# Four reorderings inside in-order engine queues of a two-block transformer kernel

## The reference

```python
h = rmsnorm(x, ffn_pre_norm[l])
u = causal_depthwise_conv(h @ w_up[l], conv_w[l], conv_b[l])
gate, up = jnp.split(u, 2, axis=-1)
y = (jax.nn.gelu(gate, approximate=True) * up) @ w_down[l]
x = x + rmsnorm(y, ffn_post_norm[l])
```

```python
shift_m, scale_m, gate_m, shift_f, scale_f, gate_f = ada_mod(c, ada_w[layer], ada_b[layer])
h = modulate(rms_norm(x, norm_gains[layer, 0]), shift_m, scale_m)
x = x + gate_m * mixer(h)
h = modulate(rms_norm(x, norm_gains[layer, 1]), shift_f, scale_f)
x = x + gate_f * swiglu(h, ffn_w_gate_up[layer], ffn_w_down[layer])
```

## Time and profile before

| | |
|---|---|
| median of 3 runs | 1071.52 us |
| time of the profiled execution | 1071.52 us |
| its span, first to last instruction | 1069.7 us |
| PE busy | 1038.4 us, 97% |
| ACT busy | 589.0 us, 55% |
| POOL busy | 153.1 us, 14% |
| granted TensorE clock, mean | 0.993 |

### The profile page before, as it was taken

How to read it: one execution, slowest core, us unless ns; L and a number is a source line. 1 busy time by engine, 2 the same in 40 slices (tenths; PEclk the granted TensorE clock), 3 DMA queues, 4 the chain that set the end, 5 groups by cost and what they waited for, 6 DMA issues and landing times.

```text
span 1069.7 us, 20330 instructions
## 1 busy us (share of the span) xinstructions
PE 1038.4 (97%) x7901; PEld 986.4 (92%) x7901; DVE 809.5 (76%) x1392; ACT 589.0 (55%) x1015; POOL 153.1 (14%) x162
## 2 busy tenths in 40 slices
PE   7999999999999999999999999999999999999997
PEld 6987798999888997899999999988899999999997
DVE  5867689999997987588999788885558567675453
ACT  6686467666536675675444445533466456544442
POOL 0000033333201200023111011200000113111010
PEclk8999999999999999999999999999999999999999
DMA  9642245777695443257998788454343536774540
GB/s 365 242 158 80 80 150 201 291 287 261 257 397 233 161 154 120 89 196 281 373 350 326 279 318 305 161 193 159 119 138 140 210 143 215 251 301 137 169 166 39
DMA packets 33684, 227.25 MB, mean 212 GB/s; under 512 B 3747, under 2 KB 4044, under 8 KB 9932
## 3 DMA queue, kind: packets, MB, share of 16 engines
q1 hardware_dynamic: 33164, 223.63, 56.6%
q0 software_dynamic: 448, 2.63, 0.6%
HBM read 225.19 MB, written 2.63 MB: 213 GB/s over the span
## 4 chain that ended last, share of the span: by engine, by line
PE 72%; DVE 18%; ACT 5%; issue 3%; DMA 1%; DVEq 0%; POOL 0%; ACTq 0%; SPq 0%
PE psum L1385 17%; PE psum L1387 17%; PE psum L1386 17%; DVE w_lo L2091 7%; DVE arena L2195 4%; PE psum L1750 3%; PE psum L1752 3%; PE psum L1751 3%; PE psum L1450 2%; PE psum L1453 2%; PE psum L1452 2%; ACT w_hi L762 2%; DVE arena L2348 1%; DVE h_lo L2356 1%; DVE hid_lo L2176 1%
## 5 line engine op out<-in xcount | busy, mean ns | idle before, releaser
L2091 DVE TENSOR_TENSOR w_lo<-raw,w_hi 128x1024 fp32r<-128x1024 f32 (+1 forms) x342 | 390.9, 1165 | 155.0 <-ACT w_hi L762 147.8
L762 ACT ACTIVATE w_hi<-raw 128x1024 fp32r<-128x1024 f32 (+1 forms) x342 | 335.7, 997 | 217.1 <-PE psum L1387 161.0
L1385 PE MATMUL psum<-h_hi,w_hi 128*128 128x256 f32 (+1 forms) x1144 | 327.8, 287 | 10.2 <-DVE w_lo L2091 4.1
L1386 PE MATMUL psum<-h_lo,w_hi 128*128 128x256 f32 (+1 forms) x1144 | 322.2, 282 | 0.0
L1387 PE MATMUL psum<-h_hi,w_lo 128*128 128x256 f32 (+1 forms) x1144 | 320.9, 280 | 0.0
L1385 PE MATMUL psum<-hid_hi,w_hi 128*128 128x256 f32 (+1 forms) x952 | 271.5, 285 | 1.8 <-DVE w_lo L2091 1.5
L1387 PE MATMUL psum<-hid_hi,w_lo 128*128 128x256 f32 (+1 forms) x952 | 269.3, 283 | 0.0
L1386 PE MATMUL psum<-hid_lo,w_hi 128*128 128x256 f32 (+1 forms) x952 | 269.2, 283 | 0.0
L1385 PEld LDWEIGHTS psum<-h_hi,w_hi 128*128 128x128 f32 x1144 | 215.3, 188 | 15.2 <-DVE w_lo L2091 6.5
L1386 PEld LDWEIGHTS psum<-h_lo,w_hi 128*128 128x128 f32 x1144 | 216.3, 189 | 0.7 <-issue 0.7
L1387 PEld LDWEIGHTS psum<-h_hi,w_lo 128*128 128x128 f32 x1144 | 216.4, 189 | 0.0
(11 more groups left out here) (266 smaller groups left out, 1183.6 us busy)
## 6 DMA issues: line engine op xcount, KB each, us to landing
arena<-in_ada SPq DMA_DIRECT2D x48, 1024.0 KB, 6.3
raw<-in_gu SPq DMA_DIRECT2D x44, 1024.0 KB, 6.4
raw<-in_ret_in SPq DMA_DIRECT2D x24, 1024.0 KB, 4.7
raw<-in_up SPq DMA_DIRECT2D x22, 1024.0 KB, 4.9
raw<-in_dn SPq DMA_DIRECT2D x32, 704.0 KB, 4.2
raw<-in_qkv SPq DMA_DIRECT2D x12, 1024.0 KB, 5.4
raw<-in_down SPq DMA_DIRECT2D x11, 1024.0 KB, 7.5
raw<-in_ret_o SPq DMA_DIRECT2D x8, 1024.0 KB, 4.8
```

Of the source, the lines that this page charges most:

```text
L762: nc.scalar.activation(w_hi[chunk % SPLIT_SLOTS][:, a:b], raw[chunk % RAW_SLOTS][:, a:b], ACT.Copy)\
L1385: nc.tensor.matmul(out, w[0], hc, start=start, stop=False, skip_group_check=True)
L1386: nc.tensor.matmul(out, w[0], lc, start=False, stop=False, skip_group_check=True)
L2091: tt(w_lo[s][:, a:b], raw[chunk % RAW_SLOTS][:, a:b], w_hi[s][:, a:b].bitcast(F32), ALU.subtract)\
```

## The change

Four orders are altered; nothing is computed otherwise, and no instruction is added or taken away.

1. **ACT, norms L0F, L1, L1F** (`start_deferred`): high 3.0 goes from behind the rounding of tile 3 to behind that of tile 4, high 3.1 and the copies of chunk 1 and of chunk 2's first tile behind that of tile 5, high 4.0 behind all eight.
2. **DVE, all five norms** (`norm_deferred`): for L0F, L1 and L1F low 2.1 moves from behind remainder 3 to behind remainder 2, low 3.0 from 4 to 5, low 3.1 from 5 to 6, low 4.0 from 6 to 7. For FFNPRE and L0 only low 4.0 moves, from 6 to 7.
3. **ACT, phase up**: `gelu` stands ahead of `conv_start` in each step, and `conv_settled(2)` ahead of the second `gelu`.
4. **PE, phase qkv**: the scores of the pairs 0 and 1 go from block 6 of chunk 4 to block 1, those of the pairs 2 and 3 from block 14 to block 11.

```diff
--- before.py
+++ after.py
@@ -1007,14 +1007,13 @@
                             hi(ph.chunk0 + 2, ahead=1)
                         if k == 2:
                             leave_first(ph, i, 0)
-                        if k == 3:
+                        if k == 4:
                             hi(ph.chunk0 + 3, ahead=0)
+                        if k == 5:
                             hi(ph.chunk0 + 3, ahead=1)
-                        if k == 4:
                             leave_first(ph, i, 1)
                             leave_first(ph, i, 2, (0,))
-                        if k == 5:
-                            hi(ph.chunk0 + 4, ahead=0)
+                    hi(ph.chunk0 + 4, ahead=0)
                 hi(ph.chunk0 + 4, ahead=1)
                 leave_first(ph, i, 2, (1,))
 
@@ -1081,8 +1080,8 @@
             gelu(Step(2))
             hi(ph.chunk0 + 5)
             round_hid(Step(2), 2)
+            conv_settled(2)
             gelu(Step(3))
-            conv_settled(2)
             round_hid(Step(3), 2)
 
             def up_step(step):
@@ -1091,9 +1090,9 @@
                     return
                 if c < ph.n and (step.i is not None or c > 4):
                     hi(ph.chunk0 + c + 1, step if step.i is not None else None, ph)
+                gelu(step)
                 if c <= ph.n:
                     conv_start(step)
-                gelu(step)
                 round_hid(step, 2)
 
             steps(act, ph.n, 8, 1, up_step)
@@ -1938,7 +1937,7 @@
                 return now
 
             HOOKS = {
-                4: {6: run((stick_scores, 0), (stick_scores, 1)), 14: run((stick_scores, 2), (stick_scores, 3))},
+                4: {1: run((stick_scores, 0), (stick_scores, 1)), 11: run((stick_scores, 2), (stick_scores, 3))},
                 5: {8: run((rotate_heads, 0))},
                 6: {8: run((rotate_heads, 1)), 10: run((stick_sums, 0), (stick_sums, 1)), 13: run((stick_sums, 2), (stick_sums, 3))},
                 7: {6: run((rotate_heads, 2)), 3: run((stick_sums, 4), (stick_sums, 5)), 10: run((stick_sums, 6), (stick_sums, 7))},
@@ -2356,7 +2355,7 @@
                         ins = stt(lo_[:, cut], tmp[:, cut], shift(k), hi_[:, cut].bitcast(F32), ALU.add, ALU.subtract)
                     ins.then_inc(h_tiles, 1)
 
-                at = {1: (3, 0), 3: (3, 1), 6: (4, 0)} if i in ROW_STAGE else {1: (2, 0), 3: (2, 1), 4: (3, 0), 5: (3, 1), 6: (4, 0)}
+                at = {1: (3, 0), 3: (3, 1)} if i in ROW_STAGE else {1: (2, 0), 2: (2, 1), 5: (3, 0), 6: (3, 1)}
                 scale(0)
                 for k in range(DT):
                     if k + 1 < DT:
@@ -2364,7 +2363,7 @@
                     rest_of(k)
                     if k in at:
                         lo(ph.chunk0 + at[k][0], ahead=at[k][1])
-                lo(ph.chunk0 + 4, ahead=1)
+                lo(ph.chunk0 + 4)
 
             row_copies(PH["w_out"], FFNPRE)
             row_residual(PH["w_out"], FFNPRE, lambda k: col("post", k))
```

## The result

The changed kernel took 1079.38 us in the median of 7 runs (1077.09 to 1083.63) against 1071.22 us (1069.57 to 1074.40, 7 runs) for the kernel before on the same chip: ratio 1.0084 [1.0058, 1.0109], slower by 8 us. A second series gave 1.0085 [1.0062, 1.0108]. The direction is the forecast's; the size is not: 1075.4 us was forecast and 1077.5 the upper end. The profiled execution took 1082.86 us with a span of 1081.1, which is 11.4 us more than before.

The account below looks back on a forecast made before the run. The prediction took PE to bound the kernel, busy 1038.4 of 1069.7 us. Scores 1.3, norms 2.4 and up 0.2 summed to +3.9 us, from 1071.52 to 1075.4 us, range 1071.7 to 1077.5.

Parts of the forecast that it names:

- What bounds the kernel: Whole kernel: PE busy 1038.4 of 1069.7 us, so reordering can win back at most 31.3 us of idle PE.
- Scores: qkv: PE waits for settle_heads ahead of the first scores, and DVE loses 0.2 us; +1.3 us, ends 1.1 and 1.5.
- Norms: Ahead of gu0, ret_in, gu1: one more scaling and remainder delay low 3.1, lengthening PE's pauses; +2.4 us, ends -0.25 and +2.8.
- gu0 gives some back: gu0: PE waits 1.1 us longer, but rounding 7's 2.34 us wait goes; net +0.6 us, ends -0.2 and 0.75.
- Up: Phase up: gelu ahead of the convolution starts changes whether POOL's product meets DVE's low halves; +0.2 us, ends -3.3 and +2.2.
- DVE busy as before: Sign in the changed profile: DVE's busy time, like ACT's, would stay as before.
- POOL's three instructions must fall somewhere: Norm of gu0: reason for a value near the upper end, their 3.71 us covering the whole rest from 482.0 on.
- norms at no cost: Rival, norms: POOL's multiplications fall behind low 3.1; norms -0.25, total +1.25, 1072.8 us; chance 0.20.
- Stretched product in up: Rival, up: POOL's product meets DVE's low halves in all steps with a modulation piece; +5.9, 1077.4 us; chance 0.13.
- Faster: Rival, up: overlapping ACT's 0.87 us wait with convolution starts removes all pauses there; total -2.45, 1069.1 us; chance 0.09.

Follow-up runs that it names:

- e_scores: Edit 4 only (the scores of qkv at their new places) against the kernel before; ratio 1.0011 [0.9998, 1.0024].
- e_after2: The changed kernel measured once more, same chip, against the kernel before; ratio 1.0085 [1.0062, 1.0108].
- e_norms: Edits 1 and 2 only (new orders in the five norms) against the kernel before; 1078.04 us against 1073.15, ratio 1.0049.
- e_busy: The changed kernel plus 16 spare matmuls ahead of chunk 3 of gu0, ret_in and gu1; ratio to the kernel before 1.0062 [1.0045, 1.0080].
- e_gelu: Edit 3 only (gelu and conv_settled(2) orders in up) against the kernel before; ratio 1.0008 [0.9994, 1.0021].
- e_early: The opposite of edit 2 (low 2.1, 3.0 and 3.1 earlier in DVE's list) against the kernel before; ratio 0.9988 [0.9976, 1.0000].

## Why the prediction was right or wrong

- **What bounds the kernel**: right. PE's pauses are where the time went, at the places named.
- **Scores, +1.3 (1.1 to 1.5)**: right in place and cause; the wait by itself, forecast as 1.19 + 0.1, is 1.26 in e_scores, and DVE's low 4.0 behind remainder 7 adds 0.3 where 0.2 was estimated. In the changed kernel DVE waits 0.18 us for ACT, and low 4.0 and low 4.1 then take 2.80 us in a row, where they took 1.21 each before:

```profile
368.30 0.48 DVE L2355 SCALAR_TENSOR_TENSOR h_lo<-arena,mod,h_hi 128x256 fp32r<-128x256 f32 x1 [0.18 <-ACT h_hi L787]
368.70 2.80 DVE L2090 TENSOR_TENSOR w_lo<-raw,w_hi 128x1024 fp32r<-128x1024 f32 x2
```

- **Norms, 0.6 + 0.85 + 0.95 = +2.4**: the mechanism was right step by step; the pauses of 2.3 to 2.6, 2.4 to 2.6 and 2.2 to 2.5 us came out as 2.66, 2.65 and 2.52. The sum was 3.4. The term that was mis-sized most is gu0's: "gu0 gives some back", which left 0.6 of 1.1. It gave nothing back: the pause grew by 1.20, and in the three profiles where the clock stayed there, e_after2, e_norms and e_busy, the lateness gathered from ahead of the pause to 50 us behind it is 1.15 to 1.23.
- **The failed step: a pause was priced at its length.** The sum has no term for what a pause does to PE afterwards. With the pauses at 2.5 us and more the clock fell behind most of them, 1.5 us each: 4.5 us in the profiled execution, 1.5 in the one of e_after2. Its share in the median isn't measured; by 3.9 + 1.0 (norms) + 0.3 (scores) + 0.7 (up) = 5.9 against the 8.2 measured it is some 2.3 us, one or two falls an execution. The one of the eight executions whose mean clock, 0.998, has room for a single stretch at half, which in the kernel before is the one near 95 us, took 1077.09 us, 5.9 above before. Without the clock's share the forecast would still have been low by 2 us, but the median, near 1077, inside the range. The range itself was too short for the prediction's own terms: the upper ends 1.5 + 2.8 + 2.2 give 1078.0, not 1077.5, and it took 0.35 for up.
- **Up, +0.2 (-3.3 to +2.2)**: inside its ends; the four profiles with edit 3 in full show 1.05, 1.05, 0.78 and 0.39, the 12 without it -0.1 in the mean, so about +0.9. POOL's product does meet DVE's low halves more often (near 186 and 190 us it takes 1.20 us, where it took 0.75, and e_gelu has 14 stretched low halves where before has 4), but the loop shows no pause for it; the 0.5 us that can be placed are at the start of the phase. This is also why "DVE busy as before" failed: 814.4 us against 809.5.
- **"POOL's three instructions must fall somewhere"**: wrong as a reason, though it gave the right number. They can fall behind low 3.1. The prediction worked out edits 1 and 2 as one and so missed that one of them, alone, takes away all three pauses.
- **Rivals**: norms at no cost, no (3.4). Stretched product in up: the stretching came, in a third of the low halves, but its price of 2 us did not. Faster, no for the four edits together; yes for edit 1, by a mechanism that the rival did not name.

## What to carry to other kernels

A pause of the matmul engine has two prices: its length, and, from about 2 us on in this kernel's norms, a chance of 1.5 us more for the half clock behind it. When a change makes pauses longer, look at the granted clock right behind them, and if the wait itself can't go, spare matmuls in it keep the clock. Take a bundle of reorderings apart before judging it: here one of four edits was worth 4 to 5 us by the medians and another one spent it, because both moved where a third engine is let in. Edit 1 alone (1068.0 and 1067.6 us) beats both kernels.

## What the runs showed of the hardware

PE's pace has a second source of variation that no order explains. Whole phases run with matmuls 0.117 or 0.120 us apart at a granted clock of 1.00. The same 60 us of gu1 in the kernel before and in e_early (PE is busy throughout in both; it makes 511 weight loads in the one and 501 in the other):

```profile
910.00:970.00 60.00, 60.00 (x512) 60.00 (x511) 41.86 (x53) 29.69 (x44) 8.69 (x11) 1.00 0.71 262
```

```profile
910.00:970.00 60.00, 60.00 (x502) 60.00 (x501) 41.36 (x53) 29.02 (x44) 8.42 (x10) 1.00 0.68 256
```

Over gu1 and dn1 this makes 2.7 us; in 5 of 17 profiles the slower pace held there, and in dn0 and ret_o it comes to 0.8 and 0.7 us. Together 4.2 us, this would make up most of the 5 us by which executions of one kernel differ, and it is one reason why a profile's difference and the medians' difference need not agree: edit 1's two profiles show 4.2 and 3.9 us, its medians 5.4 and 3.8. What chooses the pace was not found.
